# The last expert slot's rows: scatter-add to memory and read back, or a product with a zero-one matrix on TensorE, with the closing norm and gate taken by row tiles

## The chip, the cores and the metric

One core of one Trainium2 chip runs the whole program. The metric is the device time of one execution in microseconds; a kernel's time is the median of its runs. TensorE (PE) multiplies, VectorE (DVE) and ScalarE (ACT) work on SBUF and PSUM, GpSimd (POOL) here issues transfers with row indices, and SyncE (SP) issues the plain ones.

## The reference, cut to what matters

Two blocks of a transformer over 512 tokens of width 1024. The second ends in a mixture of 32 experts and a gated embedding:

```
logits = h @ w_router + b_router;  top 4 of 32 experts per token, gates = softmax(top_vals)
for each block of up to 128 (token, gate) slots that chose expert e:
    y = down_e(clamped_swiglu(up_e(h[slot_tok])));   x[slot_tok] += y * slot_gate
# the end of the program
out = x + sigmoid(rmsnorm(x, g_ple) @ w_ple_gate) * (p @ w_ple_proj)      # x: 512 x 1024
```

All arithmetic is float32, or a float32 product built of three products of rounded halves (high x high, high x low, low x high).

## The kernel before

The 512 token rows are four tiles of 128 rows, `t` = 0 to 3. Columns go in halves of 512, `n` = 0, 1 (or `j` for the halves of a transposed tile, four 128x128 transposes each). Each engine has one program, written out by hand; engines meet only at counting semaphores. PSUM has eight banks of 128x512; in the part called `late` each product has a bank and a use number of its own, and `full`, `taken`, `acquire`, `take` and `publish` wait for or raise that bank's semaphores.

**The expert loop** runs over slots. A slot is up to 128 rows of one expert; their number `nb` is known only at run time. For a slot, POOL gathers its rows, PE makes the up products (`up`), ACT and DVE form the gated activation `ea`, PE turns it (`turn_ea`) and makes the down products into banks 4 and 5 (`down`). ACT scales these by the rows' gates into `ey` (`output`), and POOL adds `ey` to the running sum `moe_sum` in memory by an indirect transfer (`scatter`; the rows' token numbers are in `idx_out`, empty places point to spare rows behind row 511). ACT may overwrite `ey`, and DVE `idx_out`, only when the scatter before has landed (semaphore `s_scat`). Each scatter runs one slot late in the loop, so two are left at the end: that of slot nb-2, issued in the last pass, and that of slot nb-1, after the loop.

**The end of the program.** While the last slot's down products run, SP loads the embedding gate's weights `w_ple_gate` as four pieces of 128x2048 into `stage` 4 to 7. After the last down product:

1. ACT copies banks 4 and 5, scaled, into `ey` (L1216); POOL scatters it (L848), waits until it has landed, and loads the whole sum back into `x` with four transfers (L876).
2. Beside this, ACT rounds the four gate pieces to `gate_hi` (L1252) and DVE makes the rests `w_lo` (L2369).
3. `norm(4)` on three engines: ACT squares and sums each tile (L904) and takes the root (L905); DVE takes the reciprocal (L1725) and scales to `xn` (L1734), two buffers; PE transposes (L1284); ACT and DVE scale one half of the columns each out of PSUM into `hT` (L920, L1718); ACT rounds to `hT_top` (L934), DVE makes `hT_low` (L1753).
4. For each tile and half, `gate` on PE: 24 products of 128x512 (three for each of eight pieces of depth 128; L1303 to L1305). ACT takes the sigmoid into `fgate` (L1260), DVE multiplies by the stored embedding `pp` and adds `x` over the whole row of 1024 (L2377, L2378), SP stores the tile (L788).

In the kernel before, PE waits for all four gate pieces and for tile t's `hT_low` before tile t's gate products, and it goes through all four tiles of step 3 before the first of step 4:

```
            norm(4)
            pe.wait_ge(s_low, len(half_no) + 4)
            for t in range(NT):
                pe.wait_ge(s_tlo, 3 * NT + t + 1)
```

Of the kernel before, what the change touches and what calls it, by code (L numbers as in the profile page):

```python
# [9 lines left out]
ALU = mybir.AluOpType  # L10
ACT = mybir.ActivationFunctionType
# [77 lines left out]
def program(nc, g, out):  # L89
# [152 lines left out]
    pick = at(R + 80 * KB, [P, NT, P], name="pick")  # L242
    bias3 = at(R + 82 * KB, [3 * NE, 3 * D], BF, name="bias3")
# [253 lines left out]
    for t in range(NT):  # L497
        for j in range(2):
            late.append((("xT", 4, t, j), (2 * t + j) % 8))
# [48 lines left out]
    s_scat, s_back = sem("scattered"), sem("sum_back")  # L548
# [115 lines left out]
    with nc.Block() as block:  # L664
# [129 lines left out]
        def _(pool):  # L794
# [76 lines left out]
            output_stands(nb - 1)  # L871
            scatter()
            pool.wait_ge(s_scat, nb * 16 + 16)
            pool.nop().then_inc(s_held, 1)
            for t in range(NT):
                pool.dma_start(x[:, t, :], acc_d[t * P:(t + 1) * P, :]).then_inc(s_back, 16)  # L876
            pool.wait_ge(s_back, 16 * NT)
# [3 lines left out]
        def _(act_e):  # L881
# [12 lines left out]
            def norm(nz, between=None, squared=None, then=None):  # L894

                for t in range(NT):
                    if nz == 0:
                        act_e.wait_ge(s_x[t], 16)
                    elif nz == 4:
                        act_e.wait_ge(s_back, 16 * NT)  # L900
                    else:
                        act_e.wait_ge(s_xr, nz * NT + t + 1)
                    k = nz * NT + t
                    link(fn(junk[:, :], x[:, t, :], ACT.Square, accum_out=stat[:, k:k + 1]))  # L904
                    fn(stat[:, 20 + k:21 + k], stat[:, k:k + 1], ACT.Sqrt, scale=1.0 / D, bias=eps[:, 0:1]).then_inc(s_sq, 1)  # L905
# [342 lines left out]
            output(nb - 1, 0, 16 * nb)  # L1248
            output(nb - 1, 1)
            for j in range(4):  # L1250
                src = half_in(act_e, nb, GATES_AT + j)
                fn(gate_hi[j][:, :], src[:, :], ACT.Copy).then_inc(s_top, 1)  # L1252
            norm(4)
            for t in range(NT):
                for n in range(2):
                    label = ("gate", t, n)
                    b = full(act_e, label)
                    if t >= 2 and n == 0:
                        act_e.wait_ge(s_out, t - 1)
                    take(fn(fgate[t % 2][:, n * CW:(n + 1) * CW], b[:, :], ACT.Sigmoid), label)  # L1260

        @block.tensor
        def _(pe):
# [422 lines left out]
            norm(4)  # L1688
            pe.wait_ge(s_low, len(half_no) + 4)
            for t in range(NT):  # L1690
                pe.wait_ge(s_tlo, 3 * NT + t + 1)
                for n in range(2):
                    b = acquire(("gate", t, n))
# [4 lines left out]
                    publish(ins, ("gate", t, n))  # L1698


        @block.vector
        def _(dve):
# [661 lines left out]
            dve.wait_ge(s_scat, 16 * nb)  # L2364
            ve.tensor_copy(idx_out[:, :], idx_all[:, bass.ds(nb - 1, 1)]).then_inc(s_ix, 1)

            for j in range(4):
                dve.wait_ge(s_top, len(half_no) + j + 1)
                tt(w_lo[GATES_AT + j][:, :], stage[GATES_AT + j][:, :], gate_hi[j][:, :].bitcast(FP), ALU.subtract).then_inc(s_low, 1)  # L2369
            norm(4)  # L2370
            dve.wait_ge(s_ppb, 16)
            for t in range(NT):
                for n in range(2):
                    taken(dve, ("gate", t, n))
                if t >= 2:
                    dve.wait_ge(s_stored[t % 2], 16 * (t // 2))
                link(tt(xo[t % 2][:, :], pp[:, t, :], fgate[t % 2][:, :], ALU.mult))  # L2377
                tt(xo[t % 2][:, :], xo[t % 2][:, :], x[:, t, :], ALU.add).then_inc(s_out, 1)  # L2378
# [21 lines left out]
```

## Time and profile before

| what | us |
|---|---|
| median of three runs | 2566.66 (2564.89 to 2574.68) |
| the profiled execution's own time | 2565.02 |
| its span, from first to last instruction | 2563.2 |
| last down product starts | 2481.41 |
| first gate product starts | 2512.38 |
| last gate product starts | 2556.50 |

Times inside the program count from the span's start. The profiled execution took 1.82 us more than its span. TensorE is busy 92% of the span and its mean granted clock is 0.950 of full speed. What the change touches begins at about 2468 us; up to there both kernels are the same program.

### The profile page before, as it was taken

What the parts mean: (1) busy time and instruction counts of PE and PEld (TensorE: products, weight loads), DVE (VectorE), ACT (ScalarE), POOL (GpSimd) and SP (SyncE); (2) the same over time, 40 slices, a digit from 0 to 9 for tenths busy, and PEclk for the clock granted to TensorE, in tenths of its full rate; (3) what the DMA queues carried; (4) which work ended last, traced back from release to release, by engine and by line L of the source; (5) the groups of instructions that cost most, each with busy time, mean ns of one, the idle gap of its engine ahead of it and who ended that gap; (6) DMA issues with size and microseconds to landing.
All of it is one profiled execution on the core that took longest, in us unless ns stands there. A gap on an engine that the chain in (4) does not pass through costs nothing.

```text
span 2563.2 us, 31147 instructions
## 1 busy us (share of the span) xinstructions
PE 2368.1 (92%) x10716; PEld 1867.0 (73%) x10716; DVE 1780.3 (69%) x2142; ACT 1334.2 (52%) x1520; POOL 149.5 (6%) x103
## 2 busy tenths in 40 slices
PE   5999988999998998677799999999999999999967
PEld 4865566888787885555577777877777787777756
DVE  7526645555624667564688888889888888988863
ACT  4353343333413236204467766776776677677643
POOL 1000000000000000001001110110111011011100
PEclk8989898999999999777799999999999999999998
DMA  8213303332121310216799999999999999999960
GB/s 312 87 66 106 141 1 99 99 99 95 41 78 66 113 66 1 91 48 230 256 357 368 360 361 369 365 361 366 367 361 362 367 365 357 370 368 360 364 227 33
DMA packets 286442, 570.40 MB, mean 223 GB/s; under 512 B 10500, under 2 KB 34983, under 8 KB 286343
## 3 DMA queue, kind: packets, MB, share of 16 engines
q1 hardware_dynamic: 273607, 523.69, 56.6%
q0 software_dynamic: 12768, 45.81, 6.5%
q8 instruction: 44, 0.72, 0.1%
q14 instruction: 23, 0.19, 0.0%
HBM read 542.70 MB, written 26.75 MB: 222 GB/s over the span
## 4 chain that ended last, share of the span: by engine, by line
PE 85%; DVE 7%; ACT 3%; issue 2%; DMA 1%; SPq 1%; DVEq 0%; POOL 0%; ACTq 0%; POOLq 0%
PE bank L1633 13%; PE bank L1635 13%; PE bank L1634 13%; PE bank L1303 6%; PE bank L1305 6%; PE bank L1304 6%; PE bank L1627 4%; PE bank L1284 4%; PE bank L1492 3%; PE bank L1493 3%; PE bank L1494 3%; PE bank L1622 2%; PE bank L1381 2%; PE bank L1363 1%; PE bank L1609 1%
## 5 line engine op out<-in xcount | busy, mean ns | idle before, releaser
L2211 DVE TENSOR_TENSOR w_lo<-stage,w_hi 128x2048 fp32r<-128x2048 f32 x364 | 818.6, 2285 | 73.2 <-ACT w_hi L1200 72.6
L1200 ACT ACTIVATE w_hi<-stage 128x2048 fp32r<-128x2048 f32 x364 | 685.5, 1912 | 228.2 <-PE bank L1635 223.9
L1633 PE MATMUL bank<-w_hi,xeT_hi 128*128 128x512 f32 x1056 | 439.3, 416 | 0.0
L1635 PE MATMUL bank<-w_hi,xeT_lo 128*128 128x512 f32 x1056 | 412.9, 391 | 0.0
L1634 PE MATMUL bank<-w_lo,xeT_hi 128*128 128x512 f32 x1056 | 412.6, 391 | 0.0
L1635 PEld LDWEIGHTS bank<-w_hi,xeT_lo 128*128 128x128 f32 x1056 | 199.0, 188 | 43.0
L1634 PEld LDWEIGHTS bank<-w_lo,xeT_hi 128*128 128x128 f32 x1056 | 199.7, 189 | 40.4
L1633 PEld LDWEIGHTS bank<-w_hi,xeT_hi 128*128 128x128 f32 x1056 | 200.5, 190 | 37.2
L1760 DVE TENSOR_TENSOR ring_low<-ring,half_top 128x2048 fp32r<-128x2048 f32 (+2 forms) x42 | 93.1, 2221 | 161.9 <-ACT half_top L943 161.6
L1305 PE MATMUL bank<-half_top,hT_low 128*128 128x512 f32 (+1 forms) x480 | 188.7, 393 | 0.0
L1633 PE MATMUL bank<-w_hi,eaT_hi 128*128 128x512 f32 x400 | 176.0, 440 | 0.0
L1303 PE MATMUL bank<-half_top,hT_top 128*128 128x512 f32 (+1 forms) x416 | 163.8, 394 | 4.0 <-DVE ring_low L1760 2.2
L943 ACT ACTIVATE half_top<-ring 128x2048 fp32r<-128x2048 f32 (+2 forms) x42 | 77.7, 1856 | 167.7 <-PE bank L1305 163.2
L1304 PE MATMUL bank<-ring_low,hT_top 128*128 128x512 f32 (+1 forms) x416 | 162.8, 391 | 0.0
L1635 PE MATMUL bank<-w_hi,eaT_lo 128*128 128x512 f32 x400 | 156.3, 391 | 0.0
L1634 PE MATMUL bank<-w_lo,eaT_hi 128*128 128x512 f32 x400 | 155.8, 389 | 0.0
L1492 PE MATMUL bank<-hT_hi,up_hi 128*128 128x512 f32 x352 | 137.8, 391 | 7.0 <-issue 7.0
L1493 PE MATMUL bank<-hT_lo,up_hi 128*128 128x512 f32 x352 | 137.7, 391 | 0.0
L1494 PE MATMUL bank<-hT_hi,up_lo 128*128 128x512 f32 x352 | 137.5, 391 | 0.0
L1216 ACT ACTIVATE ey<-bank,gates 128x512 f32<-128x512 f32 x66 | 45.5, 689 | 151.1 <-issue 111.9
L848 POOL DMA_INDIRECT moe_sum<-ey,idx_out x33 | 52.5, 1592 | 1092.1 <-ACT ey L1216 1092.1
L1627 PE MATMUL bank<-stage,ea_whole 128*128 128x512 f32 x256 | 115.1, 592 | 0.0
(414 smaller groups left out, 3860.3 us busy)
## 6 DMA issues: line engine op xcount, KB each, us to landing
stage<-in_w_up_gate SPq DMA_DIRECT2D x264, 1024.0 KB, 7.5
stage<-in_w_down SPq DMA_DIRECT2D x132, 1024.0 KB, 5.1
ring<-in_w_ada SPq DMA_DIRECT2D x12, 2048.0 KB, 8.2
ring<-in_w_up SPq DMA_DIRECT2D x22, 1024.0 KB, 7.7
ring<-in_w_in SPq DMA_DIRECT2D x10, 2048.0 KB, 7.8
ring<-in_w_out SPq DMA_DIRECT2D x4, 2048.0 KB, 13.2
ring<-in_w_down SPq DMA_DIRECT2D x4, 2048.0 KB, 8.0
stage<-in_w_ple_gate SPq DMA_DIRECT2D x4, 1024.0 KB, 7.2
```

The costliest lines, as they stand in the source:

```text
L1200: fn(w_hi[top_of(h)][:, :], src[:, :], ACT.Copy).then_inc(s_hi, 1)
L1303: mm(b, hi, wh, start=first, stop=False)
L1304: mm(b, hi, wl, start=False, stop=False)
L1305: return mm(b, lo, wh, start=False, stop=last)
L1492: mm(b[:, :], wh, hTs[0][:, k, :], start=k == 0, stop=False)
L1493: mm(b[:, :], wh, hTs[1][:, k, :], start=False, stop=False)
L1494: ins = mm(b[:, :], wl, hTs[0][:, k, :], start=False, stop=k == KT - 1)
L1627: ins = mm(bank[b][:, :], whole[:, k, :], wv[:, k, :], start=False, stop=False)
L1633: mm(bank[b][:, :], hi[:, kk, :], wh[:, k, :], start=False, stop=False)
L1634: mm(bank[b][:, :], hi[:, kk, :], wl[:, k, :], start=False, stop=False)
L1635: ins = mm(bank[b][:, :], lo[:, kk, :], wh[:, k, :], start=False, stop=kk == KT - 1)
L2211: tt(w_lo[h][:, :], stage[h][:, :], w_hi[top_of(h)][:, :].bitcast(FP), ALU.subtract).then_inc(s_lo, 1)
```

## The change

What it does:

- The scatter of slot nb-1 is left out. POOL waits only for the scatters up to slot nb-2, then loads the four tiles of `x` back, each with a semaphore of its own (`s_back[t]`).
- DVE builds `last_hot`, 128 slot rows x 512 tokens, which is 1 where the slot row belongs to the token. ACT writes the last slot's scaled rows to `ea` (`last_rows`, a half as soon as its bank is full), and PE multiplies: for each tile and half one float32 product of 128x128 by 128x512 (`("add", t, n)`, eight banks). DVE adds each product to the loaded `x` (`add`).
- ACT asks for a square root at once after the last `tiles_T`, before the last bank is full.
- Norm and gate go by tiles in a written-out order on ACT, PE and DVE; the four gate pieces are spread among them (`gate_top`, `gate_low`), and the first half of a tile's gate needs only pieces 0 and 1. The gate's sum `finish(t, n)` works on halves of 512 columns.

The diff:

```diff
@@ -240,6 +240,7 @@
     ea_whole = at(R + 68 * KB, [P, KT // 2, P], name="ea_whole")
     el = [at(R + (72 + 2 * i) * KB, [P, CW], name=f"el{i}") for i in range(2)]
     pick = at(R + 80 * KB, [P, NT, P], name="pick")
+    last_hot = at(R + 80 * KB, [P, S], name="last_hot")
     bias3 = at(R + 82 * KB, [3 * NE, 3 * D], BF, name="bias3")
     conc = at(R + 88 * KB, [P, packs["c"][1]], name="conc")
     def cc(n):
@@ -495,6 +496,9 @@
 
     late, late_uses = [], [0] * 8
     for t in range(NT):
+        for n in range(2):
+            late.append((("add", t, n), (2 * t + n) % 8))
+    for t in range(NT):
         for j in range(2):
             late.append((("xT", 4, t, j), (2 * t + j) % 8))
     for t in range(NT):
@@ -545,7 +549,9 @@
     s_route, s_slots, s_b3 = sem("routes"), sem("slot_table"), sem("expert_bias_split")
     s_pick, s_idx, s_got, s_hotu, s_hotd = (sem(n) for n in (
         "pick_built", "gather_index", "rows_gathered", "hot_up", "hot_down"))
-    s_scat, s_back = sem("scattered"), sem("sum_back")
+    s_scat = sem("scattered")
+    s_back = [sem(f"sum_back{t}") for t in range(NT)]
+    s_last, s_lhot = sem("last_rows"), sem("last_hot")
     s_out = sem("final_rows")
     s_held = sem("held")
     s_stored = [sem(f"out_stored{i}") for i in range(2)]
@@ -868,13 +874,11 @@
                 gather()
                 output_stands(i - 1)
                 scatter()
-            output_stands(nb - 1)
-            scatter()
-            pool.wait_ge(s_scat, nb * 16 + 16)
+            pool.wait_ge(s_scat, nb * 16)
+            pool.wait_ge(bank_full[4], nb + (FU[4] - 1))
             pool.nop().then_inc(s_held, 1)
             for t in range(NT):
-                pool.dma_start(x[:, t, :], acc_d[t * P:(t + 1) * P, :]).then_inc(s_back, 16)
-            pool.wait_ge(s_back, 16 * NT)
+                pool.dma_start(x[:, t, :], acc_d[t * P:(t + 1) * P, :]).then_inc(s_back[t], 16)
 
 
         @block.scalar
@@ -896,8 +900,6 @@
                 for t in range(NT):
                     if nz == 0:
                         act_e.wait_ge(s_x[t], 16)
-                    elif nz == 4:
-                        act_e.wait_ge(s_back, 16 * NT)
                     else:
                         act_e.wait_ge(s_xr, nz * NT + t + 1)
                     k = nz * NT + t
@@ -1245,13 +1247,43 @@
                 split_hi(i + 1, 2, 3)
                 output(i - 1, 1)
             tiles_T(eaT, 2 * nb + (FU[6] + 1), 3 * nb + (FU[7] + 3))
-            output(nb - 1, 0, 16 * nb)
-            output(nb - 1, 1)
-            for j in range(4):
+            fn(stat[:, 95:96], eps[:, 0:1], ACT.Sqrt)
+
+            def last_rows(n):
+
+                if n == 0:
+                    act_e.wait_ge(s_gate, 2 * nb)
+                act_e.wait_ge(bank_full[4 + n], nb + FU[4 + n])
+                act_e.nop().then_inc(s_held, 1)
+                fn(ea[:, n * CW:(n + 1) * CW], bank[4 + n][:, :], ACT.Copy, scale=gates[:, bass.ds(nb - 1, 1)]).then_inc(s_last, 1)
+
+            def gate_top(j):
+
+                if j % 2:
+                    act_e.wait_ge(bank_full[4 + j // 2], nb + FU[4 + j // 2])
+                else:
+                    act_e.wait_ge(half_read[j // 2], nb + 1)
                 src = half_in(act_e, nb, GATES_AT + j)
                 fn(gate_hi[j][:, :], src[:, :], ACT.Copy).then_inc(s_top, 1)
-            norm(4)
-            for t in range(NT):
+
+            def square(t):
+
+                act_e.wait_ge(s_xr, 4 * NT + t + 1)
+                k = 4 * NT + t
+                link(fn(junk[:, :], x[:, t, :], ACT.Square, accum_out=stat[:, k:k + 1]))
+                fn(stat[:, 20 + k:21 + k], stat[:, k:k + 1], ACT.Sqrt, scale=1.0 / D, bias=eps[:, 0:1]).then_inc(s_sq, 1)
+
+            def columns(t):
+
+                label = ("xT", 4, t, 0)
+                b = full(act_e, label)
+                for k in range(4):
+                    ins = fn(hT[:, k, t * P:(t + 1) * P], b[:, k * P:(k + 1) * P], ACT.Copy, scale=norm_cols(4, k)[0])
+                take(ins, label)
+                hT_hi(4, t)
+
+            def gate_out(t):
+
                 for n in range(2):
                     label = ("gate", t, n)
                     b = full(act_e, label)
@@ -1259,6 +1291,24 @@
                         act_e.wait_ge(s_out, t - 1)
                     take(fn(fgate[t % 2][:, n * CW:(n + 1) * CW], b[:, :], ACT.Sigmoid), label)
 
+            last_rows(0)
+            gate_top(0)
+            last_rows(1)
+            gate_top(1)
+            square(0)
+            square(1)
+            columns(0)
+            gate_top(2)
+            square(2)
+            gate_top(3)
+            square(3)
+            columns(1)
+            gate_out(0)
+            columns(2)
+            gate_out(1)
+            columns(3)
+            gate_out(2)
+            gate_out(3)
 
 
         @block.tensor
@@ -1685,17 +1735,42 @@
             turn_ea(nb - 1, 2 * nb + TK[6], 3 * nb + (TK[7] + 2))
             down(nb - 1, nb, 0, 2 * nb + (TK[6] + 1), 3 * nb + (TK[7] + 3), None)
 
-            norm(4)
-            pe.wait_ge(s_low, len(half_no) + 4)
+            pe.wait_ge(s_lhot, 1)
+            pe.wait_ge(s_last, 2)
             for t in range(NT):
+                for n in range(2):
+                    b = acquire(("add", t, n))
+                    publish(mm(b[:, :], last_hot[:, t * P:(t + 1) * P], ea[:, n * CW:(n + 1) * CW], start=True, stop=True), ("add", t, n))
+
+            def rows_T(t):
+
+                pe.wait_ge(s_xn, 4 * NT + t + 1)
+                for j in range(2):
+                    b = acquire(("xT", 4, t, j))
+                    for k in range(4):
+                        ins = tr(b[:, k * P:(k + 1) * P], xn[t % 2][:, (4 * j + k) * P:(4 * j + k + 1) * P])
+                    publish(ins, ("xT", 4, t, j))
+
+            def gate(t):
+
                 pe.wait_ge(s_tlo, 3 * NT + t + 1)
                 for n in range(2):
+                    pe.wait_ge(s_low, len(half_no) + 2 * n + 2)
                     b = acquire(("gate", t, n))
                     for k in range(KT):
                         j = 2 * n + k // 4
                         wh, wl = (a[:, k % 4 * CW:(k % 4 + 1) * CW] for a in (gate_hi[j], w_lo[GATES_AT + j]))
                         ins = three(b[:, :], of(hT_top[3])(k, t), of(hT_low)(k, t), wh, wl, k == 0, k == KT - 1)
                     publish(ins, ("gate", t, n))
+
+            rows_T(0)
+            rows_T(1)
+            gate(0)
+            rows_T(2)
+            gate(1)
+            rows_T(3)
+            gate(2)
+            gate(3)
 
 
         @block.vector
@@ -2361,21 +2436,78 @@
             rest_T(eaT, 4 * nb)
             dve.wait_ge(bank_full[5], nb + (FU[5] - 1))
             hot_row(hot[1], nb - 1, s_hotd)
-            dve.wait_ge(s_scat, 16 * nb)
-            ve.tensor_copy(idx_out[:, :], idx_all[:, bass.ds(nb - 1, 1)]).then_inc(s_ix, 1)
-
-            for j in range(4):
+            link(ve.tensor_copy(idx_f[:, 2:3], idx_all[:, bass.ds(nb - 1, 1)]))
+            ts(last_hot[:, :], cc("iota"), idx_f[:, 2:3], None, ALU.is_equal).then_inc(s_lhot, 1)
+
+            def gate_low(j):
+
                 dve.wait_ge(s_top, len(half_no) + j + 1)
                 tt(w_lo[GATES_AT + j][:, :], stage[GATES_AT + j][:, :], gate_hi[j][:, :].bitcast(FP), ALU.subtract).then_inc(s_low, 1)
-            norm(4)
+
+            def add(t):
+
+                dve.wait_ge(s_back[t], 16)
+                for n in range(2):
+                    label = ("add", t, n)
+                    b = full(dve, label)
+                    xs = x[:, t, n * CW:(n + 1) * CW]
+                    take(tt(xs, b[:, :], xs, ALU.add), label)
+                taken(dve, label)
+                dve.nop().then_inc(s_xr, 1)
+
+            def scaled(t):
+
+                k = 4 * NT + t
+                dve.wait_ge(s_sq, k + 1)
+                link(ve.reciprocal(stat[:, 40 + k:41 + k], stat[:, 20 + k:21 + k]))
+                if t >= 2:
+                    full(dve, ("xT", 4, t - 2, 1))
+                ts(xn[t % 2][:, :], x[:, t, :], stat[:, 40 + k:41 + k], None, ALU.mult).then_inc(s_xn, 1)
+
+            def columns(t):
+
+                label = ("xT", 4, t, 1)
+                b = full(dve, label)
+                for k in range(4):
+                    ins = ts(hT[:, 4 + k, t * P:(t + 1) * P], b[:, k * P:(k + 1) * P], norm_cols(4, 4 + k)[0], None, ALU.mult)
+                take(ins, label)
+                hT_lo(4, t)
+
+            def finish(t, n):
+
+                taken(dve, ("gate", t, n))
+                if t >= 2 and n == 0:
+                    dve.wait_ge(s_stored[t % 2], 16 * (t // 2))
+                cs = slice(n * CW, (n + 1) * CW)
+                link(tt(xo[t % 2][:, cs], pp[:, t, cs], fgate[t % 2][:, cs], ALU.mult))
+                ins = tt(xo[t % 2][:, cs], xo[t % 2][:, cs], x[:, t, cs], ALU.add)
+                if n:
+                    ins.then_inc(s_out, 1)
+
+            gate_low(0)
+            add(0)
+            add(1)
+            scaled(0)
+            gate_low(1)
+            scaled(1)
+            add(2)
+            columns(0)
+            gate_low(2)
+            add(3)
+            gate_low(3)
+            columns(1)
+            scaled(2)
+            scaled(3)
             dve.wait_ge(s_ppb, 16)
-            for t in range(NT):
+            finish(0, 0)
+            finish(0, 1)
+            columns(2)
+            finish(1, 0)
+            finish(1, 1)
+            columns(3)
+            for t in (2, 3):
                 for n in range(2):
-                    taken(dve, ("gate", t, n))
-                if t >= 2:
-                    dve.wait_ge(s_stored[t % 2], 16 * (t // 2))
-                link(tt(xo[t % 2][:, :], pp[:, t, :], fgate[t % 2][:, :], ALU.mult))
-                tt(xo[t % 2][:, :], xo[t % 2][:, :], x[:, t, :], ALU.add).then_inc(s_out, 1)
+                    finish(t, n)
 
 
 _INPUTS = ("x", "c", "positions", "w_ada", "b_ada", "g_attn_norm", "w_in", "g_q_latent", "g_kv_latent", "w_q_up", "w_kv_up",
```

## Rows read from the trace of the kernel before

**Rows 1.** Windows; busy us and instructions of each engine, then granted clock, DMA share, GB/s
```profile
2460.00:2482.00 22.00, 19.43 (x89) 15.28 (x87) 9.05 (x13) 6.82 (x8) 1.59 (x1) 1.00 0.42 121
2482.00:2502.00 20.00, 0.00 (x0) 0.00 (x0) 9.35 (x6) 11.07 (x10) 3.80 (x5) 0.61 0.47 131
```

**Rows 2.** The chain that ended last, from 2481: start us, us, what
```profile
2481.94 0.69 ACT ey L1216
...
2483.57 6.25 DMA moe_sum<-ey,idx_out
...
2490.42 1.70 POOL x L876 x3
...
2492.17 6.53 DMA x<-moe_sum
```

**Rows 3.** Timeline of PE, first gate product: start us, us, engine, line
```profile
2512.38 0.78 PE L1303 MATMUL bank<-gate_hi,hT_top 128*128 128x512 f32 x1
```

**Rows 4.** Timeline around the last down products, SP, POOL and ACT
```profile
2467.04 0.37 SPq L785 DMA_DIRECT2D pp<-ple_rows  x1
...
2468.68 1.59 POOL L848 DMA_INDIRECT moe_sum<-ey,idx_out  x1 [33.31 <-ACT ey L1216]
...
2478.66 0.69 ACT L1216 ACTIVATE ey<-bank,gates 128x512 f32<-128x512 f32 x1 [9.86 <-DMA moe_sum<-ey,idx_out]
```

**Rows 5.** Tile x from 2480 on: its loads from issue to landing
```profile
DMA to landing us min/median/max: 3.8/5.2/6.5
```

**Rows 6.** Timeline of PE: float32 products, transposes at full and at half clock
```profile
2417.51 3.60 PE L1627 MATMUL bank<-stage,ea_whole 128*128 128x512 f32 x8
...
2466.85 1.04 PE L1284 MATMUL bank<-cona,ea 128*128 128x128 f32 x8
...
2510.76 1.97 PE L1284 MATMUL bank<-cona,xn 128*128 128x128 f32 x8 [2.88 <-DVE xn L1734]
```

**Rows 7.** Groups by line and form, 2466 to 2563: busy us, mean ns, idle before
```profile
L1303 PE MATMUL bank<-gate_hi,hT_top 128*128 128x512 f32 x64 | 25.3, 396 | 0.0
...
L2369 DVE TENSOR_TENSOR w_lo<-stage,gate_hi 128x2048 fp32r<-128x2048 f32 x4 | 8.9, 2284 | 5.9 <-ACT gate_hi L1252 5.9
L1252 ACT ACTIVATE gate_hi<-stage 128x2048 fp32r<-128x2048 f32 x4 | 7.3, 1898 | 0.0
...
L2378 DVE TENSOR_TENSOR xo<-xo,x 128x1024 f32<-128x1024 f32 x4 | 4.9, 1226 | 0.1
...
L1753 DVE TENSOR_TENSOR hT_low<-hT,hT_top 128x1024 fp32r<-128x1024 f32 x4 | 4.8, 1219 | 1.2 <-ACT hT_top L934 1.1
...
L1718 DVE TENSOR_SCALAR hT<-bank,vec 128x128 f32<-128x128 f32 x16 | 4.5, 341 | 0.7 <-PE bank L1284 0.7
L934 ACT ACTIVATE hT_top<-hT 128x1024 fp32r<-128x1024 f32 x4 | 4.3, 1094 | 0.0
...
L1734 DVE TENSOR_SCALAR xn<-x,stat 128x1024 f32<-128x1024 f32 x4 | 3.0, 752 | 0.1
...
L2318 DVE TENSOR_TENSOR eaT_lo<-bank,eaT_hi 128x512 fp32r<-128x512 f32 x2 | 1.3, 681 | 0.0
```

**Rows 8.** Timeline of ACT: two squares in a row in norm(4)
```profile
2501.38 1.04 ACT L904 ACTIVATE junk<-x 128x1024 f32<-128x1024 f32 x1
...
2502.75 1.04 ACT L904 ACTIVATE junk<-x 128x1024 f32<-128x1024 f32 x1
```

**Rows 9.** Windows, columns as in Rows 1: where the granted clock changes
```profile
2486.00:2487.00 1.00, 0.00 (x0) 0.00 (x0) 1.00 (x2) 1.00 (x2) 0.00 (x0) 0.79 0.45 61
...
2506.00:2508.00 2.00, 1.51 (x9) 1.08 (x8) 1.54 (x5) 2.00 (x8) 0.00 (x0) 0.73 0.00 0
```

**Rows 10.** Timeline of the program's end on PE, ACT and SP
```profile
2556.50 0.39 PE L1305 MATMUL bank<-gate_hi,hT_low 128*128 128x512 f32 x1
...
2556.93 0.60 ACT L1260 ACTIVATE fgate<-bank 128x512 f32<-128x512 f32 x1 [4.84 <-PE bank L1305]
...
2560.12 0.33 SPq L788 DMA_DIRECT2D out<-xo  x1
```

## Prediction, made before the changed kernel was run

> **What bounds the kernel now.** I read the windows first. In the 22 us up to 2482 TensorE is busy 19.4 us; in the next 20 us it does nothing, and its granted clock falls [rows 1]. Then the chain that ended last, to see what fills this hole. It is one line of single steps: ACT scales the last half of the last slot's rows (0.69 us, from 2481.94), the scatter takes 6.25 us from its issue at 2483.57, POOL issues the read of the sum from 2490.42, and the fourth read lands 6.53 us after its issue, at 2498.70 [rows 2]. Norm, transposes and roundings follow, and the first gate product starts at 2512.38 [rows 3]. From there TensorE has only dense work: 192 products. The mean of 396 ns in the groups is the time of one from start to end, and they overlap [rows 7]; the last starts at 2556.50 [rows 10], so one starts every (2556.50 - 2512.38) / 191 = 0.231 us, and 0.227 without the slow first four. A half of a tile, 24 products, is 5.44 us; all eight are 43.5 us. Behind the last start 6.7 us remain to the end of the span at 2563.2. So the end has two parts that set it, 30.4 us between the last ACT step's release and the first gate product, and 43.5 us of TensorE. The change leaves the second and works on the first.
>
> **The change, part by part.** I follow what releases what. A hand-over between engines costs 0.04 to 0.1 us in the chain; I take 0.1.
>
> *The scatter taken out of the path.* POOL now waits for the scatter of slot nb-2 alone. ACT waited for that same one and went on at 2478.66; it had been issued at 2468.68 [rows 4]. In the chain 0.6 us lie between landing and the first read's issue (2489.82 and 2490.42), so the reads are issued from 2479.1. Four issues take 2.3 us. A read lands 3.8 to 6.5 us after its issue [rows 5]; the fourth had the 6.5 [rows 2], so tile 0 had less. It comes in at 2482.9 to 2485.6; I take 2483.5, near the low end for that reason. DVE was busy splitting during the four issues before, and is again, so nothing is added for that.
>
> *The last slot's rows by a product.* Bank 5 takes 25 products, about 5.7 us, so bank 4 is full at about 2476.2; ACT takes it then and no longer waits for a scatter; the half of bank 5 is ready at 2482.6 as now [rows 2]. `last_hot` (one compare of 512 columns) and the early load for the root lie on DVE and ACT before 2476, where both are idle. Then eight float32 products that before doesn't have. Nearest row: eight of the same shape and type in 3.60 us, with 0.59 for the last alone, so 0.43 us apart [rows 6]. Two are needed for tile 0: ready at about 2483.7, together with tile 0 from memory. The other six run while DVE adds. Bounds for the pair: 0.87 us, and 1.7 if they ran at half clock; the clock was still full 4 us after the down products had ended [rows 9], so the first.
> The Trainium skill (FP8 and Floating Point Precision, TensorE Precision Notes) speaks against this part: it says that true float32 takes four passes. By that a product would be 4 x 0.227 = 0.91 us, an estimate from the page, tile 0's sum would be ready 1 us later and the time about 1 us longer; this case's row shows 0.43 us, about two passes.
>
> *DVE's written order, which is now the path.* Prices: a quarter of 8.9 us for a piece's rest, 2.22; 1.22 for `hT_low`; 4 x 0.27 = 1.1 for a half's columns; 0.75 for `xn` and about 0.2 for the reciprocal; a 512-column operation with one operand in PSUM 0.68 [rows 7], so 1.5 for a tile's two adds with their signal. This last is a new form; its upper bound is the row for 1024 columns, 1.23 per half. ACT: 1.37 from one square to the next [rows 8], 1.1 for `hT_top`, 7.3 / 4 = 1.83 for a piece's rounding [rows 7].
> From 2483.5: adds of tile 0 to 2485.0; ACT's square and root to 2486.5; `xn` of tile 0 to 2487.5 (the adds of tile 1 are under the square); rest of piece 1 to 2489.7; `xn` of tile 1 to 2490.6; adds of tile 2 to 2492.1; columns of tile 0 to 2493.2; ACT's `hT_top` to 2494.3. Here it forks. DVE makes `hT_low` of tile 0 by 2495.6, and the first gate product can start, 17 us earlier than now. ACT rounds piece 2 by 2496.1; DVE its rest to 2498.4, adds of tile 3 to 2499.9, rest of piece 3 to 2502.1. That is when the second half of tile 0's gate may start. The first half takes 5.44 us from 2495.7 at full clock. But TensorE has idled and will have had only 16 small transposes since 2486; the clock fell about 5 us after the last product [rows 9] and came back about 4.6 us after the next work, begun at 2502.5 (the window's 0.73 lies between the levels of 1.2 and 2.4 GHz). Cold products cost up to twice as much, so the loss is between nothing and 0.47 x 4.6 = 2.2 us; I take 1.6, nearer the upper since the transposes are sparse. It ends at 2502.7, so the late piece is just hidden.
>
> *From 2502.7 on* TensorE does seven halves, 38.1 us, and transposes tiles 2 and 3 between them, 1.04 us each at full clock (1.97 at half) [rows 6]: the last product starts at 2542.7. The inputs are early: `xn` of tiles 2 and 3 on DVE by 2507.5, wanted at 2508.1; `hT_low` of tile 1 by 2505.6, wanted at 2509. Tiles 2 and 3 have a tile's 10.9 us of gate products as cover for their 5 us of columns and roundings; without it they would cost those 5 us each.
>
> *The end.* `finish` works on 512 columns. Two operations of about 0.69 replace two of 1.23 [rows 7] after the last sigmoid, 1.1 us less; of the 6.7 us 5.6 remain, with the same store [rows 10]. The extra instructions of the earlier halves lie under gate products.
>
> **Sum:** 2542.7 + 5.6 = 2548.3 against 2563.2: 14.9 us less. By the execution's own time, 2565.02 - 14.9 = 2550.1; that execution lay 1.64 us under the median shown, so against the median: 2566.66 - 14.9 = **2551.8**.
>
> **Rivals.** What the kernel can tell from no change is about 0.5%, 12.8 us, so everything above 2553.8 counts as the same.
> 1. *DVE's order runs slower than my prices.* Every step of it from 2483.5 to 2502.1 lies on the path, beyond the 0.6 us that the cold first half hides. With the adds at their upper bound of 1.23 the end moves 3.6 us (six halves on the path at 0.55 more, and 0.3 by which those of tile 1 outlast the square above them); with tile 0 landing at 2485.6, 2 us; with the full cold loss, 0.6. All together 2558.0; the adds alone carry it over the bound of 2553.8, and so do the two others together. For it: an operation in PSUM and SBUF with an addition in place isn't in before; the steps alternate between two engines, and 0.1 us more at some twenty instructions is 2 us. Against it: the 0.68 row has the same operands.
> 2. *The memory still sets the start.* The indirect transfer is no longer waited for, but the read is; were it as slow as the scatter of slot nb-2, 9.8 us from 2468.68 [rows 4], tile 0 would come at 2489 and put all 5.5 us later: 2557.3. For it: that scatter, slower than the 6.25 us of the last one, in the same place of the program. Against it: SP's last load began at 2467.04 [rows 4], beside that scatter and 12 us before the reads, whose longest took 6.5 us.
> 3. *The slower side: the clock stays down.* The hole becomes a sparse stretch, and if TensorE stayed at 1.2 GHz through gate products, each would cost 0.2 us more. From 14.9 / 0.2 = 75 of the 192 on, the kernel is slower than before; all of them would be 38 us, 2590. For it: the clock fell once more between transposes around 2511. Against it: full clock was back within 2 us of the first gate product at 2512.38, and the new order has no gap inside the gate longer than a fraction of a us.
> 4. *It doesn't do what it says.* For the hole to stay, something else would have to hold the first gate product to 2512. Even now a rounding and four rests behind 2482.6 are over by 2482.6 + 1.83 + 4 x 2.22 = 2493.3, so I leave this 1 in 100.
>
> **How the numbers follow.** The forecast with its own spread holds 70 in 100; rival 1 beyond the bound 20; rival 2, 4; rival 3, 3; the rest, with rival 4, 3. The likeliest is 2551.8. Below it: tile 0 at its earliest and no cold loss bring 1.1 us, adds a little under the row and shorter hand-overs another 2, and the lowest of the runs shown lies 1.8 us under their median: low end 2547.5. Above: rival 1 in full, 2558. Faster by over 0.5%: 0.72. Same: 0.24, mostly rival 1. Slower: 0.04.
>
> **What would show it.** Right: no scatter after 2470, ACT's last rows at 2481.9 as now, reads issued at 2479; adds at 0.7 us each, starting before 2484; the first gate product between 2495 and 2497; a stall of under 1 us before the 25th; then no gap on TensorE over 0.3 us to the end; last product's start at 2543 and 5.6 us behind it. Wrong: adds above 0.9 us; a gate start after 2499, by tile 0's landing or by DVE; a pause before tile 0's second half with `w_lo` as releaser; a granted clock under 1 beyond the first half.

## The result, and the profile after

The changed kernel takes 2554.65 us (median of six runs, 2552.99 to 2559.29) against 2567.99 us (six runs): a ratio of 0.9945, 95% interval 0.9929 to 0.9960. By the ratio that is 14.1 us less, by the two medians 13.3 us. The forecast was 14.9 us less and 2551.8 us, with a range of 2547.5 to 2558. A second timing of the same kernel, in the experiments below, gave 0.9942 (0.9928 to 0.9955).

The profiled execution was the slowest of its six, 2559.29 us with a span of 2557.4, and its trace has to be read with that in mind: only 5.8 us less than before. The difference lies in the part that both kernels share. The first rows gathered for an expert come at 1220.64 in the kernel before, at 1229.58 here, and at 1222.85 in the second execution of this same kernel.

```profile
1229.58 1.77 POOL L850 DMA_INDIRECT rows<-hn_rows,idx_in  x1 [31.29 <-DVE idx_in L2349]
```

So I count from a landmark inside the program, ACT's scaling of the last half of the last slot's rows, to the end of the span, and call it the tail: 2563.2 - 2481.94 = 81.3 us before [rows 2], 2557.4 - 2490.32 = 67.1 us here, 14.2 us less. The profiled execution of the second timing gave 67.5. The two agree within 0.01 us up to the first gate product; the 0.45 us between them arise behind it, where the granted clock was half for more products in the second. So the start of the gate can be compared between single executions within a tenth of a us, a tail only within about half a us, and the whole time not at all at this size.

The timeline of POOL after: no scatter comes after the one at 2477.06, and the reads are issued 2.45 us before the tail begins.

```profile
2477.06 1.58 POOL L854 DMA_INDIRECT moe_sum<-ey,idx_out  x1 [33.31 <-ACT ey L1218]
2487.87 2.22 POOL L881 DMA_DIRECT2D x<-moe_sum  x4 [9.24 <-DMA moe_sum<-ey,idx_out]
```

The timeline of DVE after (start us, us, line, in brackets the idle time before and what ended it) is the path that the prediction followed: adds (L2454), `xn` (L2465), rest of piece 1 (L2445), `xn` of tile 1 (behind the first cut mark below), adds, columns (L2472), `hT_low` (L1828), rest of piece 2, adds, rest of piece 3.

```profile
2492.35 1.48 DVE L2454 TENSOR_TENSOR x<-bank,x 128x512 f32<-128x512 f32 x2 [2.84 <-PE bank L1743]
2494.07 1.48 DVE L2454 TENSOR_TENSOR x<-bank,x 128x512 f32<-128x512 f32 x2 [0.24 <-PE bank L1743]
...
2495.91 0.75 DVE L2465 TENSOR_SCALAR xn<-x,stat 128x1024 f32<-128x1024 f32 x1
2496.57 2.29 DVE L2445 TENSOR_TENSOR w_lo<-stage,gate_hi 128x2048 fp32r<-128x2048 f32 x1
...
2499.64 1.28 DVE L2454 TENSOR_TENSOR x<-bank,x 128x512 f32<-128x512 f32 x2
2501.08 1.13 DVE L2472 TENSOR_SCALAR hT<-bank,vec 128x128 f32<-128x128 f32 x4 [0.16 <-DVE x L2454]
2503.33 1.23 DVE L1828 TENSOR_TENSOR hT_low<-hT,hT_top 128x1024 fp32r<-128x1024 f32 x1 [1.12 <-ACT hT_top L936]
2505.13 2.29 DVE L2445 TENSOR_TENSOR w_lo<-stage,gate_hi 128x2048 fp32r<-128x2048 f32 x1 [0.58 <-ACT gate_hi L1267]
2507.34 1.28 DVE L2454 TENSOR_TENSOR x<-bank,x 128x512 f32<-128x512 f32 x2
2508.78 2.29 DVE L2445 TENSOR_TENSOR w_lo<-stage,gate_hi 128x2048 fp32r<-128x2048 f32 x1 [0.16 <-DVE x L2454]
```

What the reader is to see: DVE waited 2.84 us for the first product, not for memory; then its only idle times of more than 0.25 us are 1.12 and 0.58 us at hand-overs to ACT. The timeline of PE, against [rows 3, 6, 10]:

```profile
2491.15 7.11 PE L1743 MATMUL bank<-ea,last_hot 128*128 128x512 f32 x16 [0.97 <-ACT ea L1258]
2498.09 1.04 PE L1334 MATMUL bank<-cona,xn 128*128 128x128 f32 x8
2499.78 1.09 PE L1334 MATMUL bank<-cona,xn 128*128 128x128 f32 x8 [0.65 <-DVE xn L2465]
2504.61 0.54 PE L1353 MATMUL bank<-gate_hi,hT_top 128*128 128x512 f32 x1 [3.74 <-DVE hT_low L1828]
```

The last gate product starts at 2551.42.

The windows (columns as in [rows 1]) show the granted clock in this execution: full through the adds and transposes, half from the first gate products on, behind 3.7 us in which TensorE idled.

```profile
2500.00:2504.00 4.00, 0.87 (x8) 0.63 (x6) 2.72 (x7) 1.76 (x2) 0.00 (x0) 1.00 0.00 0
2504.00:2506.00 2.00, 1.39 (x4) 1.17 (x5) 1.42 (x2) 2.00 (x3) 0.00 (x0) 0.73 0.00 0
2506.00:2508.00 2.00, 2.00 (x6) 1.54 (x6) 2.00 (x3) 1.97 (x4) 0.00 (x0) 0.50 0.00 0
```

In the second execution of the same kernel the clock fell about 3 us earlier, inside that idle stretch, 11 to 13 us behind the tail's begin (2484.97 there), with the same work on TensorE up to that point:

```profile
2496.00:2498.00 2.00, 0.00 (x0) 0.00 (x0) 0.88 (x5) 1.11 (x2) 0.00 (x0) 0.70 0.00 0
```

### The profile page after: what moved, and what is told of

The parts are those of the page before. It is cut to its first block, busy times and chain, and to the rows that moved or that the text cites. A ratio compares the mean times of both kernels' runs of the same rounds, so it can differ in the third digit from the quotient of the medians.

```text
span 2557.4 us, 31210 instructions
## 1 busy us (share of the span) xinstructions
PE 2378.7 (93%) x10732; PEld 1871.2 (73%) x10732; DVE 1787.9 (70%) x2159; ACT 1335.4 (52%) x1521; POOL 147.9 (6%) x102
## 4 chain that ended last, share of the span: by engine, by line
PE 85%; DVE 8%; issue 2%; ACT 2%; DMA 1%; SPq 1%; DVEq 0%; POOL 0%; ACTq 0%
PE bank L1683 13%; PE bank L1685 13%; PE bank L1684 13%; PE bank L1353 6%; PE bank L1354 6%; PE bank L1355 6%; PE bank L1677 4%; PE bank L1334 4%; PE bank L1542 3%; PE bank L1543 3%; PE bank L1544 3%; PE bank L1431 2%; PE bank L1672 2%; PE bank L1413 1%; PE bank L1659 1%
```

## The experiments

Times in us behind the tail's begin; the 25th gate product opens the second half of tile 0. All edits are against the changed kernel. The three columns of times come from one profiled execution each; the last column is the median of the whole time and the number of executions behind it. Six of the kernels ran once, so for them only the tail says anything. Ratios are against the kernel before as run beside each; its median was 2569.79 us beside the two parts and 2570.67 us beside the last two kernels.

| kernel | first gate product | 25th | tail | whole time (executions) |
|---|---|---|---|---|
| before | 30.4 | 36.7 | 81.3 | 2567.99 (6) |
| changed | 14.3 | 21.5 | 67.1 | 2554.65 (6) |
| the same again | 14.3 | 21.9 | 67.5 | 2554.68 (5) |
| order without product | 20.1 | 25.7 | 71.0 | 2559.42 (10) |
| product without order | 24.6 | 30.1 | 75.1 | 2562.80 (10) |
| no early root | 15.3 | 22.4 | 68.0 | 2556.19 (1) |
| whole-row finish | 14.3 | 21.2 | 67.9 | 2557.82 (1) |
| rounded products | 13.3 | 21.2 | 66.9 | 2552.46 (1) |
| reads held | 16.3 | 23.9 | 69.5 | 2555.84 (1) |
| piece 1 early | 12.7 | 19.9 | 65.5 | 2555.87 (1) |
| kept busy | 14.3 | 20.8 | 66.5 | 2555.42 (1) |
| reordered | 11.5 | 17.3 | 63.1 | 2551.00 (5) |

**The order without the product.** The scatter of the last slot is back, no add products; everything else as in the change but that ACT and DVE split all four gate pieces before norm. "Order" is therefore short for four things: the row tiles in turn, a wait for each tile's read by itself, the early root and the half-width finish.

```diff
-            pool.wait_ge(s_scat, nb * 16)
+            output_stands(nb - 1)
+            scatter()
+            pool.wait_ge(s_scat, nb * 16 + 16)
...
-                act_e.wait_ge(s_xr, 4 * NT + t + 1)
+                act_e.wait_ge(s_back[t], 16)
```

> The tail is counted from ACT's scaling of the last half of the last slot's rows to the end of the span: 81.3 us before, 67.1 us in the changed kernel. This run keeps the scatter and the read back through memory, and takes the rest of the change (row tiles in turn, half-width finish, early root, a semaphore for each tile's read); the four gate pieces are split while memory works. Theory (both parts pay, the tile order more): the first gate product waits only for tile 0's way through norm, so it starts about 20 us after the tail's begin (30.4 before, 14.3 in the changed kernel), the tail is 73 us, and the time 8 us less than before. Rival (the product is what pays, the order only follows from it): first gate product later than 25 us, tail above 77 us.

Measured: 2559.42 us, ratio 0.9963 (0.9952 to 0.9973); tail 71.0, 2 us shorter than I expected. The first gate product came at 20.1 as expected; what I had too dear was what follows it. No product ran at half clock (24 products took 5.6 us, 7.2 in the changed kernel), and the stretch behind the last product was 0.35 us shorter. The clock had come back to full just behind the transposes of tiles 0 and 1, 1.6 us before the gate began. In the chain that ended last the scatter and one read, instead of four, are all that stands before ACT's first square:

```profile
2488.14 6.09 DMA moe_sum<-ey,idx_out
2494.28 0.55 issue
2494.83 3.68 DMA x<-moe_sum
2498.53 1.16 ACT junk L1271 x2
```

These parts together take 10.3 us off the tail without the product. The rival falls. The traces say where most of it comes from. ACT's first square starts 12.0 us behind the tail's begin, 16.8 before: waiting for one read instead of four is worth 4.8 us. From that square to the first gate product it takes 8.1 us instead of 13.7. Of these 5.6 us 1.28 are a load of ACT's table, which in the kernel before stands between the first square and its root:

```profile
2499.89 1.28 ACT L905 ACT_TABLE_LOAD   x1
```

The rest, about 4.3 us, is the way from there of one tile (with the next one's transposes beside it) in front of the gate, instead of four tiles. In the gate the clock gives 0.7 us and the transposes between tiles take 1.8 back; the end is 1.1 us shorter by the half-width finish. The parts weren't run one by one.

**The product without the order.** `last_rows` and the adds as in the change, then `norm(4)` and all gates as before, with whole-row finish.

```diff
-            rows_T(0)
-            rows_T(1)
-            gate(0)
...
+            norm(4)
+            pe.wait_ge(s_low, len(half_no) + 4)
+            for t in range(NT):
+                gate(t)
```

> Only the product in place of the last scatter, with all four tiles normed and transposed before the first gate product and whole-row finish, as before; all four gate pieces must be ready before the gate. Theory: about 6 us less than before, tail 75 us, since DVE now has adds and the rests of three pieces in front of norm; first gate product 24 us after the tail's begin. Rival (the memory round trip was the whole loss): tail below 70 us, close to the changed kernel's 67.1.

Measured: 2562.80 us, ratio 0.9978 (0.9965 to 0.9990); tail 75.1, first gate product at 24.6, as expected. The product with the early root, which this run keeps, takes 6.2 us off. The two runs give 10.3 + 6.2 = 16.5 us, the whole change 14.2. Both contain the early root, so a part of the difference is counted twice. On top of the order the product is worth 71.0 - 67.1 = 3.9 us. The traces divide it: ACT's first square comes 8.4 us earlier; from there to the first gate product it takes 2.6 us more, since DVE's rest of piece 1 and adds of tile 2 now lie between; the half clock in the first half costs 1.6 and the end 0.35.

**No early root.**

```diff
-            fn(stat[:, 95:96], eps[:, 0:1], ACT.Sqrt)
```

> The changed kernel without the root that ACT computes while it waits for bank 4. The table load of 1.28 us then comes behind the first square, on the path to the first tile's rows: tail 67.1 + 1.2 = 68.3 us. If the norm of tile 0 weren't on the path it would stay at 67.1.

Measured: tail 68.0, 0.9 us more than the first execution of the changed kernel and 0.5 more than the second. The timeline of ACT shows the load behind the first square:

```profile
2491.09 1.28 ACT L1273 ACT_TABLE_LOAD   x1
```

The first gate product comes 1.0 us later, which is well clear of the 0.01 us by which it repeats. The prediction placed the early load before 2476, where ACT is idle, which is right, but gave the edit no value of its own; by the gate's start it is worth 1.0 us.

**Whole-row finish.**

```diff
+                if n == 0:
+                    return
...
-                cs = slice(n * CW, (n + 1) * CW)
+                cs = slice(0, D)
```

> The changed kernel with the closing multiply and add over whole rows of 1024 instead of halves. Behind the last sigmoid two operations of 1.23 us stand for two of 0.69: tail 67.1 + 1.1 = 68.2 us, give or take 0.4 for the last store; first gate product unchanged at 14.3.

Measured: tail 67.9, 0.9 us more (expected 1.1, within the spread named). From the last product's start to the end it takes 7.06 us instead of 5.98, so the 1.1 us are there; two fewer products at half clock hid 0.2 of them.

**Rounded products.**

```diff
-    last_hot = at(R + 80 * KB, [P, S], name="last_hot")
+    last_hot = at(R + 80 * KB, [P, S], FR, name="last_hot")
+    ea_r = at(R + 56 * KB, [P, D], FR, name="ea_r")
...
```

ACT then writes `ea_r` instead of `ea`, and the products read it.

> The changed kernel with the zero-one matrix and the last slot's rows as rounded halves instead of full float32, so the low part of the last slot's rows is left out. Theory (a full float32 product takes four passes, the two rows of the trace for each product being two passes each): 8 rows instead of 16, each 0.23 us after the other, so all eight end 5.3 us earlier; tile 0's second product 1.3 us earlier, which moves the adds until tile 0 from memory bounds them; tail between 66.0 and 66.8 us. Rival (the products are hidden behind the read of tile 0): tail unchanged at 67.1 us.

Measured: tail 66.9. The first half of the theory holds. The timeline of PE has 8 rows, 0.24 us apart, where the changed kernel has 16, (7.11 - 0.60) / 15 = 0.43 us apart:

```profile
2484.54 2.08 PE L1744 MATMUL bank<-ea_r,last_hot 128*128 128x512 f32 x8 [0.97 <-ACT ea_r L1259]
...
2492.15 1.97 PE L1335 MATMUL bank<-cona,xn 128*128 128x128 f32 x8 [1.97 <-DVE xn L2466]
```

The second half doesn't. The adds started 0.6 us earlier, still released by the first product, and the first gate product came 1.0 us earlier; but the tail shrank by 0.2 us against the first execution of the changed kernel and by 0.6 against the second. TensorE's granted clock fell sooner, about 8 us behind the tail's begin instead of 12 and 14.6, so that already tile 1's transposes took 1.97 us, where they took 1.09 in both executions of the changed kernel, and the gate began at half clock:

```profile
2490.00:2496.00 6.00, 2.14 (x10) 1.57 (x8) 4.68 (x10) 2.31 (x6) 0.00 (x0) 0.65 0.00 0
```

By the distance of their starts, eight gate products ran at half clock in the changed kernel, ten when it ran again, eleven here. The fall came earlier than in either execution of the changed kernel. How much of the 1.0 us it took back is less sure, 0.8 us by one execution and 0.3 by the other.

**Reads held.**

```diff
-            pool.wait_ge(bank_full[4], nb + (FU[4] - 1))
+            pool.wait_ge(bank_full[5], nb + FU[5])
```

> The changed kernel with the four reads of the sum held until the last down product has ended, so issued about 3.1 us later, 0.6 us after the tail's begin instead of 2.45 before it. It shows how much room the reads had. Theory (a first read lands 3.7 us after its issue, so tile 0 was in memory 1.2 us after the tail's begin and the product at 2.0 bounds the adds): adds start 4.4 us after the tail's begin instead of 2.0, tail 67.1 + 2.4 = 69.5 us. Rival (the read of tile 0 takes 5.1 us, the median of the four, and bounds the adds already): tail 70.2 us.

Measured: tail 69.5, adds at 4.4, as the theory had it. DVE now names memory as its releaser:

```profile
2488.82 1.29 DVE L2454 TENSOR_TENSOR x<-bank,x 128x512 f32<-128x512 f32 x2 [5.22 <-DMA x<-moe_sum]
```

The reads were issued at 0.44 and tile 0 was there at 4.4, 4.0 us later. In the changed kernel they were issued at -2.45, so by the same 4.0 us tile 0 is there at about 1.5 (an estimate), and the product at 2.0 is what DVE waits for. Memory has half a us of room and no more. The gate began only 2.0 us later, since the later adds no longer waited for TensorE; the other 0.4 of the tail's 2.4 us are two more products at half clock, as in the second execution of the changed kernel.

**Piece 1 early.**

```diff
             gate_top(0)
-            last_rows(1)
             gate_top(1)
+            last_rows(1)
```

and on DVE `gate_low(1)` before `add(0)`.

> The changed kernel with piece 1 of the gate's weights rounded by ACT before, not behind, the last half of the last slot's rows, and its rest made by DVE before the adds: both in stretches in which these engines were idle. Theory (DVE's written order is the path from tile 0's adds to the gate): 2.2 us of DVE leave the path, first gate product 12.1 us after the tail's begin instead of 14.3, tail 67.1 - 2.2 = 64.9 us. Rival (the granted clock gives it back, as with the rounded products, where the first gate product came 1.0 us earlier and the tail shrank by 0.2): tail 66 to 67 us with a half clock over more of the first half.

Measured: tail 65.5, first gate product 12.7: 1.6 us less, not 2.2, since DVE then waits 0.49 us for tile 1's root. Eight products ran at half clock, as in the first execution of the changed kernel, so the clock took nothing of it. DVE's order is the path.

**Kept busy.**

```diff
             rows_T(1)
+            b = acquire(("gate", 0, 0))
+            for _ in range(4):
+                mm(b[:, :], last_hot[:, 0:P], ea[:, 0:CW], start=True, stop=True)
             gate(0)
```

> The changed kernel with four more full float32 products (3.5 us, results never read) on TensorE between tile 1's transposes and the first gate product, where it otherwise idles 3.7 us. Theory: the granted clock stays at 1.0 through the first half, so its products are 0.227 us apart from the start and the half takes 5.5 us instead of 7.2; but the rest of piece 3 is ready only 20.8 us after the tail's begin, so the second half starts 0.7 us earlier and no more, with a wait of about 1 us before it: tail 66.4 us. Rival (the cold start costs nothing, being hidden behind piece 3): tail 67.1.

Measured: tail 66.5, 25th product at 20.8. The granted clock stays full. The first window is that of the gate's start, the line below it the wait that appears before the second half:

```profile
2501.00:2507.00 6.00, 5.74 (x24) 4.43 (x24) 5.27 (x5) 5.50 (x10) 0.00 (x0) 1.00 0.00 0
```

```profile
2507.77 0.50 PE L1353 MATMUL bank<-gate_hi,hT_top 128*128 128x512 f32 x1 [0.78 <-DVE w_lo L2448]
```

So in the changed kernel the half clock costs 21.46 - 20.81 = 0.65 us net in its first execution and 1.1 in its second (21.92); the rest of it lies over the wait for piece 3.

**Reordered, and the changed kernel again.** On ACT, PE and DVE:

```diff
@@ ACT
             gate_top(0)
-            last_rows(1)
             gate_top(1)
+            last_rows(1)
+            gate_top(2)
...
@@ PE
             rows_T(0)
+            add(3)
             rows_T(1)
@@ DVE
             gate_low(0)
+            gate_low(1)
             add(0)
             add(1)
             scaled(0)
-            gate_low(1)
             scaled(1)
-            add(2)
-            columns(0)
+            columns(0, lambda: add(2))
```

> The changed kernel in another order. ACT rounds pieces 0 and 1 before the last half of the last slot's rows and piece 2 right behind it; DVE makes the rests of 0 and 1 before the adds, then scales tiles 0 and 1, does tile 0's columns, adds tile 2 while ACT rounds, makes tile 0's low part, and only then piece 2; TensorE transposes tile 0 before the last two add products. Theory: first gate product 11.7 us after the tail's begin (14.3 in the changed kernel), rest of piece 3 at 17.4 (20.8), and TensorE idle only about 1.4 us before the gate, so the clock stays up: 25th gate product at 17.5 (21.5), tail 63.1 us, 4 us less than the changed kernel and 18 less than before. Rival (the clock falls all the same): first half 7.2 us, tail 64.6.

> The changed kernel once more, on the same chip and in the same rounds as the reordered one: 14.2 us less than before in the tail, so a ratio near 0.9945; tail 67.1 us.

Measured: reordered 2551.00 us (2546.99 to 2552.61), ratio 0.9921 (0.9907 to 0.9935), tail 63.1, 25th product at 17.3; the changed kernel again 2554.68 us, ratio 0.9942, tail 67.5. The intervals of the ratios overlap a little, the tails differ by 4.0 to 4.4 us, far more than the 0.45 us between two executions of one kernel: 18.2 us less than before against 13.7 to 14.2. TensorE's idle time before the gate is down to 1.37 us and the clock stays up, as the theory said. That the smaller gap is what keeps it up fits this run and the one kept busy, but the work before the gap moved too and wasn't varied by itself:

```profile
2497.48 0.50 PE L1353 MATMUL bank<-gate_hi,hT_top 128*128 128x512 f32 x1 [1.37 <-DVE hT_low L1833]
```

```profile
2497.00:2504.00 7.00, 6.40 (x27) 5.01 (x28) 6.84 (x9) 4.54 (x11) 0.00 (x0) 1.00 0.00 0
```

## Why the prediction was right

Its steps against the trace, in us behind the tail's begin (2481.94 in the prediction, 2490.32 after):

| step | predicted | measured |
|---|---|---|
| tile 0 in `x` from memory | 1.6 | about 1.5 (reads held) |
| adds of tile 0 begin | 1.6 | 2.0 |
| `xn` of tile 0 | 5.6 | 6.3 |
| `hT_top` of tile 0 | 12.4 | 13.0 |
| first gate product | 13.8 | 14.3 |
| rest of piece 3 | 20.2 | 20.8 |
| second half begins | 20.8 | 21.5 |
| last product starts | 60.8 | 61.1 |
| end of the span | 66.4 | 67.1 |

The path was the one predicted: the scatter left it, DVE's written order became it, the first half of tile 0's gate hid the late piece 3, and from there TensorE ran without a gap that the sum hadn't (1.03 us from the last product of a tile to the first of the next, with the transposes between). The adds took 0.69 us each, the nearer of the two bounds. That the tail came out within 0.7 us is in part luck: the gate's start was 0.5 us late and the end 0.4 us too long, while from the second half to the last product TensorE took 0.4 us less than the sum, mostly because a set of transposes adds 0.9 us to it and not 1.04. The time itself is a weaker check. The prediction counts as faster only what is more than 0.5% below before; the ratio 0.9945 is just beyond that, and its interval reaches across it.

- **The mis-sized term** is the price of a float32 product. The prediction read eight rows of `bank<-stage,ea_whole` [rows 6] as eight products, 0.43 us apart. The code makes four products there (`fill` loops over `KT // 2`), and the trace shows each as two rows. The changed kernel's 16 rows for eight products say the same, and the rounded run's eight rows. A product is 0.87 us, not 0.43. DVE's first add waited for the first product until 2.03 instead of 1.6, and its next ones for 0.2 and 0.24 us more. This is most of the 0.8 us by which `xn` of tile 0 was late; 0.5 of it was left at the gate's start. The Trainium skill (FP8 and Floating Point Precision, TensorE Precision Notes) gives four passes for true float32; by it the prediction had reckoned 0.91 us and about 1 us more in the time. The trace agrees with the page on the price of a product, 0.87 us beside 0.91, and the sentence that preferred the row had misread the row. The gate's start moved by 0.5 us, less than the 1 us reckoned.
- **The clock** was sized well and in part by luck: 1.6 us of loss was predicted in the first half, measured are 7.2 - 5.44 = 1.7 us and, in the second execution, 2.2. The prediction took the clock as falling some 5 us behind the adds, during the transposes. It stayed full through them and fell 14.6 us into the tail, just as the gate began, in one execution, and at about 12 in the other. The traces don't say what moved it by 3 us.
- **The end** behind the last product was 6.0, not 5.6 us. The halves gave what was reckoned (1.1 us behind the last product by the whole-row run); the last store took 3.5 us from its issue to the end of the span where it had taken 3.1 before. 0.3 to 0.4 us more appear in every kernel without the last scatter and not in the order without product, which has it; why is open.
- **Rival 1** (DVE slower than its prices) was wrong in size and right in place: taking 2.2 us of DVE off the path brought 1.6, as piece 1 early shows. **Rival 2** (memory) is out by half a us: the reads held 2.9 us moved the adds by 2.4. **Rival 3** (a clock that stays down) didn't happen: 8 and 10 products of 192 ran at half clock, far from the 75 it needed.

One thing the prediction didn't price is how the gain divides: it spoke of the scatter first. The order's four parts alone are 10.3 us, the product alone 6.2. Without the finish (1.1) and the table load (1.3) an estimate of 7.9 us remains for not waiting for all four tiles, still the larger part.

## What to carry to other kernels

When a chain through memory ends a program, look first at what waits for all of something and needs only a part: here letting each row tile go on by itself, from its read on, brought more than taking the memory trip away. Once the big wait is gone, the written order of the engine between two others is the path; look for its pieces that can move into stretches where it idles, which brought a further 4 us. Before taking a price per instruction from a group, count the instructions that the code issues there: one product can be two rows.

## What the runs showed of the hardware that was not expected

- A float32 product of 128x128 by 128x512 is two matmul rows, 0.43 us each at full clock; the same as rounded halves is one row of 0.23 to 0.24 us. A float32 transpose of 128x128 is one row, eight of them 1.04 us.
- Making TensorE's work shorter in a sparse stretch can cost its clock: with the add products at about a quarter of their price the granted clock fell 3.7 and 6.5 us earlier than in the two executions of the changed kernel, and took back 0.3 to 0.8 of the 1.0 us gained; with 3.5 us of unused products added it never fell. When it falls isn't fixed by the kernel: two executions with the same work differed by 3 us.
- Transposes alone brought the clock back: in the kernel before TensorE did nothing between the down products and its transposes from 2502.51 on (1.04 us for eight at full clock, 1.97 at half), and the granted clock rose from half to full at about 2507 [rows 9], before any gate product; in the order without product it rose 4.0 us behind the first transpose, 1.6 us before the gate.
- The part that both kernels share differed by up to 8.4 us between three profiled executions (start of the tail at 2481.94, 2484.97 and 2490.32), while the tail of the one kernel that was profiled twice repeated within 0.5 us. What in that part varies I didn't follow.
